# A diffusion backbone on one core: first modulation weights in idle memory, the first norm reordered, a filter spectrum moved into the projection

## The reference

```
mod = silu(c) @ w_ada[li] + b_ada[li]          # 6 x 1024 columns; context: silu(c_ctx)
sh1, sc1, g1, sh2, sc2, g2 = split(mod)
h = rmsnorm(x, norm1[li]) * (1 + sc1) + sh1    # rmsnorm: x * rsqrt(mean(x*x) + 1e-6) * w
p = h @ w_in[li]                               # one projection for four mixers
A: differential attention   B: Hyena long convolution   C: 2-D Fourier mixing   D: gated DeltaNet
x += g1 * (sum_n sigmoid(h @ Wg_n) * (y_n @ Wb_n)) @ w_o
x += g2 * relu(h2 @ w_mlp1)**2 @ w_mlp2
# B: filter = small MLP with sines over positions, times a decay, divided by the sum of its
#    magnitudes, then an rfft: the filter's spectra, two orders for each layer
```

## Time and profile before

| | us |
|---|---|
| median of 3 runs | 1945.58 |
| lowest, highest | 1943.26, 1947.38 |
| span of the profiled execution, first to last instruction | 1946.3 |
| PE busy | 1873.7 (96%) |
| DVE, ACT, POOL busy | 1284.9, 788.5, 608.5 |

### The profile page before, as it was taken

One profiled execution on the slowest core, in us unless ns is written; L12 is line 12 of the kernel. 1 busy time (PEld: TensorE's weight loads), 2 busy tenths in 40 slices (PEclk: granted clock), 3 DMA queues, 4 the chain that ended last, 5 costly groups with the idle time before them and its releaser, 6 DMA issues.

```text
span 1946.3 us, 32006 instructions
## 1 busy us (share of the span) xinstructions
PE 1873.7 (96%) x11146; PEld 1525.9 (78%) x11146; DVE 1284.9 (66%) x2122; ACT 788.5 (41%) x1627; POOL 608.5 (31%) x553
## 2 busy tenths in 40 slices
PE   6999899999999999999999999999998899999999
PEld 2556788767588888877888887787787789999999
DVE  4754867666856755358765776759686655567574
ACT  2325633356243333333222232356535545445453
POOL 3433243722312111163200223444555521143030
PEclk8999899999999999999999999999999999999999
DMA  6433111232234443344555556233214335554554
GB/s 226 139 107 105 38 56 55 87 121 80 84 130 152 130 161 118 95 134 160 185 173 186 174 194 196 87 87 87 77 44 136 104 109 176 177 168 156 180 183 140
DMA packets 210925, 252.98 MB, mean 130 GB/s; under 512 B 11715, under 2 KB 176900, under 8 KB 209796
## 3 DMA queue, kind: packets, MB, share of 16 engines
q1 hardware_dynamic: 207088, 235.01, 38.2%
q10 hardware_dynamic: 3732, 16.60, 2.3%
HBM read 245.29 MB, written 6.29 MB: 129 GB/s over the span
## 4 chain that ended last, share of the span: by engine, by line
PE 73%; issue 10%; DVE 8%; POOL 5%; ACT 4%; DMA 1%; ACTq 1%; DVEq 0%; POOLq 0%
PE psum L660 58%; PE psum L655 13%; POOL whl L1544 2%; DVE big L2570 2%; PE psum L766 1%; POOL big L3537 1%; ACT whl L1535 1%; ACT big L1783 1%; ACT big L1786 1%; PE psum L628 1%; DVE hhl L2739 1%; DVE big L2579 1%; POOL big L1634 1%; DMA big<-in_hy_table_dram 1%; DVE big L2722 1%
## 5 line engine op out<-in xcount | busy, mean ns | idle before, releaser
L660 PE MATMUL psum<-hhl,whl 128*128 128x512 f32 (+1 forms) x4416 | 826.6, 346 | 11.6 <-DVE hhl L2739 4.3
L660 PEld LDWEIGHTS psum<-hhl,whl 128*128 128x128 f32 x4416 | 693.3, 190 | 132.4 <-issue 24.8
L1535 ACT CAST whl<-raw 128x512 fp32r<-128x512 f32 x656 | 374.1, 618 | 811.6 <-PE psum L660 806.6
L1544 DVE TENSOR_TENSOR whl<-raw,whl 128x512 fp32r<-128x512 f32 x480 | 333.6, 736 | 315.3 <-ACT whl L1535 314.4
L660 PE MATMUL psum<-bigr,whl 128*128 128x512 f32 (+1 forms) x2688 | 474.9, 337 | 1.5 <-DVEq L3314 0.7
L660 PEld LDWEIGHTS psum<-bigr,whl 128*128 128x128 f32 x2688 | 412.8, 190 | 57.2 <-issue 2.2
L1544 POOL TENSOR_TENSOR whl<-raw,whl 128x512 fp32r<-128x512 f32 x176 | 233.6, 1349 | 377.5 <-ACT whl L1535 359.0
L655 PE MATMUL psum<-big 128*128 128x128 f32 (+8 forms) x1572 | 245.7, 326 | 17.9 <-DMA big<-in_hy_w_dram 5.4
L655 PEld LDWEIGHTS psum<-big 128*128 128x128 f32 (+4 forms) x1572 | 164.5, 175 | 77.3 <-issue 51.8
L3537 POOL TENSOR_TENSOR big<-big,tmp 128x512 f32<-128x512 f32 (+1 forms) x64 | 64.5, 1021 | 341.3 <-DVE tmp L3311 340.7
L660 PE MATMUL psum<-whl,hhl 128*128 128x512 f32 x672 | 160.1, 396 | 11.0 <-POOL whl L1544 9.1
(11 more groups left out here) (187 smaller groups left out, 1524.9 us busy)
## 6 DMA issues: line engine op xcount, KB each, us to landing
raw<-in_w_mlp_dram SPq DMA_DIRECT2D x128, 512.0 KB, 3.8
raw<-in_w_in_dram SPq DMA_DIRECT2D x88, 512.0 KB, 3.7
big<-in_w_ada_dram SPq DMA_DIRECT2D x88, 512.0 KB, 5.1
raw<-in_w_gate_dram SPq DMA_DIRECT2D x64, 512.0 KB, 3.5
raw<-in_w_branch_dram SPq DMA_DIRECT2D x32, 512.0 KB, 3.5
raw<-in_w_ada_dram SPq DMA_DIRECT2D x24, 512.0 KB, 5.3
raw<-in_w_o_dram SPq DMA_DIRECT2D x16, 512.0 KB, 3.5
hy_spectra<-big ACTq DMA_DIRECT2D x2, 2560.0 KB, 9.3
```

What stands on the lines that cost most here:

```text
L660: m = nc.tensor.matmul(o_, a(p_), b(q_), start=first and i == 0, stop=last and i == 2, skip_group_check=shared)
L1535: nc.scalar.copy(whl[:, r, 0, ks], raw_of(n)[:, ks]).then_inc(S["hi_ready"], 1)
L1544: ins = eng.tensor_tensor(whl[:, r, 1, ks], raw_of(n)[:, ks], whl[:, r, 0, ks].bitcast(F32), ALU.subtract)
```

## The change

It touches only layer 0 up to its first projection blocks.
- The 8 MB of the first modulation weights no longer pass through the ring. They are loaded by five transfers into memory that has no use yet: a part of the arena, `whl` and `hhl` (groups 0 and 1; 2 and 3; 4 and 5; 6; 7), each with a semaphore of its own. The first projection strips are issued right behind them.
- SP issues `tab` and the tokens first. ACT's queue takes the row vectors of layer 0 ahead of the filter loads, and the three filter tables right behind them, before silu.
- The tokens are transposed before the modulation. ACT makes all 8 squares (to `x_sq`), POOL adds them; `rstd` is made before group 3. POOL multiplies all 8 parts by `rstd` as soon as it is there. After `amp`, one instruction with two scalars (times `amp`, plus shift) per half finishes a part: even parts on DVE, odd ones on POOL. ACT's high part is then a plain copy of 512 columns, DVE's low part a plain subtraction.
- The first two projection strips are split between rows 6 and 7 (ACT) and columns 6 and 7 (DVE).
- Spectrum (0, 0) stands behind the last turn; its nyquist row and scale (0, 1) move between the halves of the first pair; spectrum (0, 1) moves behind chunk 4, the taps of layer 1 from chunk 4 to 5, and the first store of spectra behind the gates.

```diff
@@ -258,6 +262,10 @@
         hy_back = y[:, FN, 3, :].rearrange("p (a s t) -> p a s t", a=2, s=2)
         HYB["u0"] = y[:, HY].rearrange("p h t -> p (h t)").rearrange("p (m n) -> p m n", m=NT)
 
+        mod_raw = [v.rearrange("p (k c) -> p k c", k=KD) for v in
+                   (arena[:, 8192:12288], whl_plain[:, :], hhl_plain[:, 0:4096], hhl_plain[:, 4096:6144],
+                    hhl_plain[:, 6144:8192])]
+        x_sq = carve((KD, T), at=12288)
         f_w1, f_w2, f_s, f_arg, f_turns, f_feats, f_inv = carve((P,), (P,), (L,), (L,), (L,), (L,), (BR_W,), at=6144)
         f_inv = [f_inv, carve((BR_W,), at=6144 + 2 * P + L)]
...
-                    mod_turn(li, g - 1)
+                    m.then_inc(filled if kh else unit_done, 1)
+
+            def first_mod(g):
+
+                bank = unit()
+                at, c0 = mod_part(g)
+                pe.wait_ge(mod_loaded[at], 16)
+                for k in range(KD):
+                    m = mm(bank[32 * (k % 4):32 * (k % 4) + 32, 0:STRIP], csil[:, k, :],
+                           mod_raw[at][:, k, c0:c0 + STRIP], k < 4, k >= 4)
+                m.then_inc(unit_done, 1)
+                if g:
+                    mod_turn(0, g - 1)
 
             def mod_turn(li, g):
                 pe.wait_ge(S["modrow_ready"], mod_place(li, g) + 1)
...
             def start_():
+                def x_turned(ks):
+                    for k in ks:
+                        b = fill(("x", k))
+                        turn(b, [stage[:, m, k * P:(k + 1) * P] for m in range(NT)]).then_inc(filled, 1)
+
                 pe.wait_ge(consts_loaded, 16)
                 columns(0)
+                pe.wait_ge(x_loaded, 32)
+                x_turned(range(4))
                 filter_angles(0)
+                x_turned(range(4, KD))
                 pe.wait_ge(S["cT_ready"], 2)
...
+                first_mod(0)
+                filter_angles(1)
+                first_mod(1)
+                columns(1)
+                first_mod(2)
+                pe.wait_ge(S["sq_summed"], 1)
+                mm(fill(("ms", 0, 0)), ones, tmp[:, 1, :]).then_inc(filled, 1)
+                filter_taps(0, 0)
+                first_mod(3)
+                filter_taps(0, 1)
+                first_mod(4)
+                first_mod(5)
+                filter_scale(0, 0)
+                first_mod(6)
+                first_mod(7)
                 mod_turn(0, FIRST_MODS - 1)
-                filter_scale(0, 1)
+                filter_spectrum(0, 0)
...
                     if li == 0:
+                        if chunk == 1:
+                            filter_nyquist(0, 0)
+                            filter_scale(0, 1)
                         if chunk == 7:
                             gates()
                         if chunk == 4:
+                            filter_spectrum(0, 1)
                             filter_nyquist(0, 1)
-                        if chunk in (4, 12):
+                        if chunk in (5, 12):
                             filter_taps(1, chunk // 12)
...
+            sp.dma_start(stage[:, 0:2, :], ctx[0].rearrange("(m p) d -> p m d", p=P)).then_inc(x_loaded, 16)
+            sp.dma_start(stage[:, 2:4, :], x[0].rearrange("(m p) d -> p m d", p=P)).then_inc(x_loaded, 16)
+            for g in (0, 2, 4, 6, 7):
+                at, _ = mod_part(g)
+                src = w_ada[0][:, STRIP * g:STRIP * g + mod_raw[at].shape[2]]
+                sp.dma_start(mod_raw[at], src.rearrange("(k p) n -> p k n", p=P)).then_inc(mod_loaded[at], 16)
+                if g == 0:
+                    load_rows(1, sp)
             for li in range(DEPTH):
                 for n in range(first_strip["dn", li], first_strip["merge", li]):
-                    if li and n == first_strip["dn", li] + RAW:
+                    if n == first_strip["dn", li] + RAW:
                         load_vecs(li)
                     load_strip(n)
...
+                load_rows(0, act)
                 load_filter()
+                load_filter_tables()
                 act.wait_ge(S["cols_ready"], 1)
                 for s_ in range(2):
                     step(f(csil[:, :, s_], cols[:, 0, 1, 36 + 8 * s_:44 + 8 * s_], ACT.Silu), S["cT_ready"])
...
+                for k in range(4):
+                    x_copy(k)
+                    x_square(k)
+                for k in range(4, KD):
+                    x_copy(k)
                 filter_sine(0)
...
+                mod_row(0, 0)
+                for k in range(4, KD):
+                    x_square(k)
+                filter_sine(1)
+                log_exp_tables()
+                mod_row(0, 1)
+                mod_row(0, 2)
+                b = filled_bank(act, ("ms", 0, 0))
+                rsqrt(rstd[:], b, D, S["rstd_ready"], after=lambda: give_fill(act, ("ms", 0, 0)))
+                mod_row(0, 3)
+                filter_taps(0, 0)
+                mod_row(0, 4)
+                mod_row(0, 5)
+                filter_taps(0, 1)
+                mod_row(0, 6)
                 for i in range(RING):
                     split_hi(act, split_strips[i])
+                mod_row(0, 7)
+                for k in range(KD):
+                    nm, count = hn_ready(0, k)
+                    act.wait_ge(S[nm], count)
+                    copy(hhl[:, 0, k, :], HN[0][:, k, :]).then_inc(S["hhi_ready"], 1)
...
                     silu(0)
                     silu(1)
                     ahead(2)
-                    keep_spectra(0)
                     ahead(3)
                     gates()
+                    keep_spectra(0)
                     filter_taps(1, 0)
                     silu(2)
...
+                mod_cols(0, 0)
+                mod_cols(0, 1)
+                columns(1)
+                mod_cols(0, 2)
+                filter_cut(0, 0)
+                filter_sums(0, 0)
+                mod_cols(0, 3)
+                filter_cut(0, 1)
+                mod_cols(0, 4)
+                mod_cols(0, 5)
+                filter_sums(0, 1)
+                filter_scale(0, 0)
+                mod_cols(0, 6)
                 for i in range(RING):
                     split_lo(dve, split_strips[i])
+                mod_cols(0, 7)
+                amps(0, 0)
+                first_norm()
+
+            def first_norm():
+                hn = HN[0]
+
+                def scaled(k):
+                    dve.wait_ge(S["xa_ready"], k + 1)
+                    for s_ in range(2):
+                        sl = slice(s_ * L, (s_ + 1) * L)
+                        ins = V.tensor_scalar(hn[:, k, sl], hn[:, k, sl], amp[:, 0, 0, k, s_:s_ + 1],
+                                              mod[:, 0, k, s_:s_ + 1], MUL, ADD)
+                    ins.then_inc(S["hn_dve"], 1)
+
+                def low(k):
+                    nm, count = hn_ready(0, k)
+                    dve.wait_ge(S[nm], count)
+                    dve.wait_ge(S["hhi_ready"], k + 1)
+                    signals(dve, V.tensor_tensor(hhl[:, 1, k, :], hn[:, k, :], hhl[:, 0, k, :].bitcast(F32), SUB),
+                            S["h_ready"])
+                scaled(0)
+                scaled(2)
+                low(0)
+                low(1)
+                scaled(4)
+                low(2)
+                low(3)
+                scaled(6)
+                low(4)
+                low(5)
+                low(6)
+                low(7)
+                dve.wait_ge(S["h_ready"], KD)
+                filter_spectrum(0, 0)
+                filter_nyquist(0, 0)
                 filter_scale(0, 1)
+                layer_vecs(0)
...
+            def first_norm():
+                hn = HN[0]
+                for k in range(1, KD):
+                    pool.wait_ge(S["x_ready"], 2 * k + 2 if k < 4 else KD + k + 1)
+                    a = x_sq[:, 0, :] if k == 1 else tmp[:, 1, :]
+                    step(G.tensor_tensor(tmp[:, 1, :], a, x_sq[:, k, :], ALU.add),
+                         S["sq_summed"] if k == KD - 1 else pool_step)
+                pool.wait_ge(S["rstd_ready"], 1)
+                for k in range(KD):
+                    G.tensor_tensor(hn[:, k, :], xT[:, k, :], rstd[:], ALU.mult).then_inc(S["xa_ready"], 1)
+                pool.wait_ge(S["xa_ready"], KD)
+                pool.wait_ge(S["amp_ready"], 1)
+                for k in range(1, KD, 2):
+                    for s_ in range(2):
+                        sl = slice(s_ * L, (s_ + 1) * L)
+                        ins = G.tensor_scalar(hn[:, k, sl], hn[:, k, sl], amp[:, 0, 0, k, s_:s_ + 1],
+                                              mod[:, 0, k, s_:s_ + 1], ALU.mult, ALU.add)
+                    ins.then_inc(S["hn_pool"], 1)
+                pool.wait_ge(S["h_ready"], KD)
...
```

More of the change, by code:

```diff
@@ L158, in sbr @@
             return es.enter_context(nc.sbuf_tensor(name, shape, F32R))
+        with nc.sbuf_tensor("whl_plain", [P, RING * 2 * KS * STRIP], F32) as whl_plain:
+            pass
         whl = sbr("whl", [P, RING, 2, KS, STRIP])
```

(53 more changed lines are left out.)

175 lines of the change are left out of this document (51 added, 124 removed).

## The result

The changed kernel takes **1964.15 us** (median of 4 runs, 1960.38 to 1965.33), the kernel before 1945.05 on the same chip: ratio **1.0089, 95% interval 1.0075 to 1.0103**. It is slower by 17 us by this ratio (19 by the medians); 1944.6 was forecast, in a range that ended at 1950.5. The profiled execution has a span of 1963.3.

A forecast was written before the change was run, and what follows sets the result against it. PE, busy 96% of the span, was taken as the bound, so only its earlier exit from the first 100 us counts. Gain 66 - amp is 1.0 at 65; 1946.3 - 1.0, less 0.7, gives 1944.6 us, range 1939.5 to 1950.5.

The forecast's parts named there:

- the rest of the 1946 us keeps its order: Work after the first pair and its moved spectrum, layer 1 included: taken as unchanged, so no time was added there.
- the second rival: ACT's row 6 waits behind magnitudes and DVE's sums: amp at 70 to 72, loss 4 to 6 us, 1950.6; chance 0.16.
- The mark: Reference for gain: first pair ending at 88.0 us is level; page's span 1946.3 taken as 0.7 above the runs' median.
- Loads: Start of layer 0: PE ready for modulation group 0 at 20.5 us, between sums giving 19.5 and 21.6.
- To the first taps: From group 0 to the first filter taps: 32.5 us against 29.57 before, with 1.5 added to DVE's angle for POOL.
- To amp: First taps to amp, including a 9.6 us serial wait: 63.6 at high clock, 69.0 at low; 65 taken, 68.83 before.
- From amp to the pair: POOL's odd parts at 1.1 us each, first spectrum, nyquist row in time by 1 us: pair ends at amp + 22.
- Second spectrum: Moved behind the first pair: costs PE 7.0 us there, less a 1.2 us stall at layer 1's first taps that goes.
- Behind the pair: Store of first spectra behind the gates costs 0, or 1 us late; the rest of the kernel keeps its order.
- The first rival: Clock stays high from the first groups, sums uncontended: amp 59.5 to 61, gain 5 to 6.5 us, 1940; chance 0.24.
- POOL and DVE did not shut each other out in the scaling: Rival after amp: DVE's 8 scalings alternate with POOL's 8, bank 1.3 late, gain -0.3 us, 1945.9; chance 0.06.
- the change does what it says: Denied by a rival: weights come no earlier than PE asks, freed POOL work hides other filter work; 1945.6, chance 0.04.

The follow-up runs named there:

- a1: Changed kernel with ACT's modulation row 6 freed of the second filter's magnitudes, which go behind row 7: 1958.0 us, 1.0057 of the kernel before.
- e2: Changed kernel with POOL's additions 4 to 7 held until both filter angles are made, sum of squares behind modulation 3: 1959.1 us, 1.0070 of the kernel before.
- g1: Changed kernel with 8 more DVE MEMSETs and unread matmuls, 4 ahead of modulation 2, 3 ahead of modulation 1's turn: 1953.95 us, 1.0040 of the kernel before.
- d2: Changed kernel with row 6 freed of the filter's work and 8 more DVE MEMSETs at the start: 1951.85 us, 1.0029 of the kernel before.
- b3: Kernel before with only the second filter's spectrum moved behind chunk 4 and the next layer's taps one pair later: ratio 1.0038.
- d1: Changed kernel with 8 small MEMSETs more on DVE at its very start: 1959.44 us, 1.0074 of the kernel before.
- c2: Kernel c1 with 4 unread matmuls added in PE's wait for modulation 2's weights: 1946.69 us, 1.0002 of the kernel before.
- c1: Changed kernel with row 6 freed, POOL's additions 4 to 7 held until both angles are made, 8 more DVE MEMSETs: 1951.6 us, 1.0032 of the kernel before.

## Why the prediction was wrong

Three steps failed: the choice of 65 for amp between a sum of 63.6 and one of 69.0, which leaned to the higher clock; the size of POOL's effect on DVE's angle; and "the rest of the 1946 us keeps its order", which put layer 1 at nothing. A part of the loss stood in it as the second rival, the serial wait, with a chance of 0.16 and a price of 4 to 6 us; clock, angle and layer 1 come on top of it. Its steps, in order:

- **The mark.** It set the page's span of 1946.3 beside the times of the runs and found it 0.7 above their median. But the span of a timed execution is about 2 us below its time (1942.81 and 1940.9 in the rounds of a1). So the traced execution, taken as typical, was some 2.6 us longer than the typical one.
- **Loads.** Group 0 at 22.41 against 20.5, beyond the upper bound of 21.6. Of the two sums, the one by the rule of the Trainium skill (DMA: Bandwidth & Descriptors, Queues, rings and completion order) was the nearer, and 22.41 fits it; no run separates this rule from other reasons for a late landing. Group 2's weights came only at 29.68, which the sum did not have; it hid under DVE's angle, and PE stood still for 3.88 us.
- **To the first taps.** 36.19 instead of 32.5. The loads give 1.9, the angle 2.4: 1.5 us were added for POOL, with 3.4 as the bound, and it was 3.9 (7.3 against 3.4); 0.6 were saved elsewhere. The bound came from a factor, 6.21 against 2.87, of instructions of 0.69 us; but each takes about as long as POOL's beside it, so shorter ones grow by more: 0.32 to 1.30, 0.43 to 1.45. e2 confirms it for the angle. The Trainium skill (SBUF — State Buffer, Who interferes with whom) has a scalar instruction wait in the two-port mode until GpSimd's instruction has ended; 1.30 us each beside POOL's four in 5.30, the three ending 0.15 us after one of POOL's, agrees. I had weighed this rule for the scaling and not for the angle. In the scaling the trace does not show it: DVE's eight take 0.40 to 0.65 us beside POOL's 1.05.
- **To amp.** The sum at the lower clock was right: 26.9 us from the first taps to the turn of modulation 5, measured 27.6; the serial wait 9.6, measured 10.85. 69.0 + 3.7 + 0.7 + 1.25 is 74.65. The step that failed is the choice of 65 between a sum of 63.6 and one of 69.0: 4.0 of the 9.65 us by which amp is late. I expected the clock high early and rising in groups 4 and 5; it fell at 27.6, in the wait for group 2, and rose at 58.3. g1 measures 4.5 us for that; the wait for row 6, which the low sum contains and which was left to a rival, is worth 5.5 us from turn to amp (a1, d2) and brings a second fall of the clock.
- **From amp to the pair.** 24.15 us instead of 22: POOL's 1.05 us each and the nyquist row in time were right; 2.7 us are the first spectrum at the fallen clock, of which 0.7 are given back since it starts 1.3 us ahead of amp and not 0.6. With row 6 free it is 23.2 (a1, d2), where PE waits 0.85 and 0.47 us for DVE, so 1.2 us were missing from the 22 anyhow.
- **Second spectrum.** 7.0 us forecast, less a stall of 1.2: 5.8. The traces have 7.05 (5.26 late before it, 12.31 behind it; b3: -1.78 and 5.29). The stall was misread: between 96.65 and 102.19 stand twelve instructions of 0.43 us, not ten, so it was 0.4 and not 1.2, and none of it shows as a gain.

```profile
96.49 5.77 PE L655 MATMUL psum<-big 128*128 128x512 f32 x12
```

- **Behind the pair.** "The rest of the 1946 us keeps its order" was true of the order and false of the time: 5.3 us in layer 1, from 8 instructions fewer on DVE (d1; by time its gain is 2.9 us with intervals that overlap). No step of the forecast looked there.
- The first rival's clock came true with matmuls added (c2), its time of 1940 in no run. POOL and DVE did not shut each other out in the scaling, and the change does what it says.

The terms of the loss of 17.0 us in the trace: amp 9.65 later than taken, pair 2.15 longer, 0.95 for the second spectrum (7.05 instead of 5.8), less the 0.6 that come back before 260 us, and rounding, less the 1.0 gain forecast: 11.75; and 5.3 in layer 1.

## What to carry to other kernels

When an order is rewritten by hand, follow each queue's first late instruction, not the busiest engine: one small copy on ACT behind a block of filter work cost 5.5 us between turn and amp, and the 10 us saved on POOL bought nothing against it. Where a sum differs by 5 us between two levels of the clock, the likelier is the one that the waits ahead suggest; each wait that the change adds to PE speaks for the lower one, though not surely (a1's taps ran fast behind much the same waits). One trace is one execution: set its span and mean clock beside those of the timed runs before taking it as typical. And an order that is the same in a later layer is not the same in time: half a microsecond on DVE became five.

## What was not expected of the hardware

- DVE beside POOL's additions of 1.27 us: an instruction with one tensor as source (128x256) took 1.30 us instead of 0.32, one with two 1.45 instead of 0.43, one of four columns 1.21 instead of 0.16. Each took about POOL's time, whatever its own. Those that read PSUM (0.75 us in layer 1) were not slowed beside POOL's splits.
- A pause of 0.4 to 0.5 us on DVE, followed about 0.7 us later by 8 KB on the instruction queue, moves with the number of instructions ahead of it.
- Work for PE that nobody reads can pay: 4 matmuls (3.7 us) in a wait brought 5 us and more (c2 against c1), 7 of them 6.6 us by ratio (g1 against d1), and 3 or 4 in the kernel before nothing.
